# The modulation products of a two-block transformer step: matrix-vector work moved from TensorE to GpSimd between the feed-forward tiles

## The reference, cut to what matters

```
sh_l, sc_l, g_l = split(silu(c)     @ w_mod[l] + b_mod[l], 3)
sh_c, sc_c, g_c = split(silu(c_ctx) @ w_mod[l] + b_mod[l], 3)
hl = xl * (1.0 + sc_l) + sh_l
```

## Time and profile before

| | |
|---|---|
| median of 3 runs (lowest, highest) | 3065.2 us (3062.55, 3065.78) |
| span of the profiled execution; no other time of its own is given | 3064.5 us |
| TensorE busy in the span | 98% |
| VectorE, ScalarE, GpSimd busy in the span | 54%, 44%, 1% |
| mean granted clock of TensorE | 0.993 of full speed |
| the stage with the up tiles, from the span's start | about 791 us to 1306 us |
| instructions in the span | 48560 |

### The profile page before, as it was taken

How to read it: one execution, slowest core, us unless ns; L and a number is a source line. 1 busy time by engine, 2 the same in 40 slices (tenths; PEclk the granted TensorE clock), 3 DMA queues, 4 the chain that set the end, 5 groups by cost and what they waited for, 6 DMA issues and landing times.

```text
span 3064.5 us, 48560 instructions
## 1 busy us (share of the span) xinstructions
PE 2991.3 (98%) x19912; PEld 2540.5 (83%) x19912; DVE 1668.5 (54%) x2561; ACT 1352.7 (44%) x2084; POOL 43.7 (1%) x84
## 2 busy tenths in 40 slices
PE   8999999999899999999999999999999999999997
PEld 7888876898688888788888887788888998889996
DVE  6666666443766666664463325554563564257754
ACT  5333334434455555454453224444442562255543
POOL 1000000000000000000000000000000000000000
PEclk9999999999999999999999999999999999999998
DMA  7666655446766666745552222222233442234442
GB/s 255 231 212 216 220 192 216 139 163 264 272 232 220 220 234 249 279 160 187 180 184 97 94 85 83 83 79 88 88 132 110 165 165 83 97 123 149 152 157 105
DMA packets 73800, 510.18 MB, mean 166 GB/s; under 512 B 8325, under 2 KB 8465, under 8 KB 19601
## 3 DMA queue, kind: packets, MB, share of 16 engines
q1 hardware_dynamic: 63504, 435.74, 41.4%
q0 software_dynamic: 10112, 71.73, 5.8%
HBM read 503.23 MB, written 6.55 MB: 166 GB/s over the span
## 4 chain that ended last, share of the span: by engine, by line
PE 93%; DVE 4%; ACT 1%; DMA 1%; issue 0%; SPq 0%; ACTq 0%; DVEq 0%
PE bank L777 21%; PE bank L721 16%; PE bank L720 8%; PE bank L1500 6%; PE bank L1502 6%; PE bank L1501 6%; PE bank L920 3%; PE bank L921 3%; PE bank L922 3%; PE bank L952 2%; PE bank L1060 2%; PE bank L818 2%; PE bank L819 1%; PE bank L820 1%; PE bank L1127 1%; PE bank L1538 1%
## 5 line engine op out<-in xcount | busy, mean ns | idle before, releaser
L2322 DVE TENSOR_TENSOR ring_f32r<-ring_f,high_f32r 128x1024 fp32r<-128x1024 f32 (+1 forms) x738 | 830.1, 1162 | 751.7 <-ACT high_f32r L1675 728.1
L1675 ACT CAST high_f32r<-ring_f 128x1024 fp32r<-128x1024 f32 (+1 forms) x644 | 609.4, 995 | 836.8 <-PE bank L777 461.4
L721 PE MATMUL bank<-hyz_f32r,high_f32r 128*128 128x512 f32 x2112 | 743.4, 398 | 1.0 <-DVE hyz_f32r L2322 1.0
L720 PE MATMUL bank<-hyz_f32r,ring_f32r 128*128 128x256 f32 x2008 | 562.6, 280 | 3.0 <-DVE hyz_f32r L2322 2.0
L777 PE MATMUL bank<-hyz_f32r,high_f32r 128*128 128x512 f32 (+1 forms) x2016 | 536.7, 343 | 4.3 <-DVE hyz_f32r L2322 2.1
L721 PEld LDWEIGHTS bank<-hyz_f32r,high_f32r 128*128 128x128 f32 x2112 | 391.8, 188 | 101.7 <-issue 15.3
L777 PE MATMUL bank<-hyz_f32r,ring_f32r 128*128 128x512 f32 (+1 forms) x1184 | 411.8, 348 | 0.0
L777 PEld LDWEIGHTS bank<-hyz_f32r,high_f32r 128*128 128x128 f32 x2016 | 349.9, 191 | 48.1 <-issue 2.8
L720 PEld LDWEIGHTS bank<-hyz_f32r,ring_f32r 128*128 128x128 f32 x2008 | 378.9, 189 | 8.5 <-DVE hyz_f32r L2322 2.7
L1500 PE MATMUL bank<-hyz_f32r,high_f32r 128*128 128x512 f32 (+1 forms) x1024 | 359.3, 351 | 3.0 <-DVE ring_f32r L2322 3.0
L1502 PE MATMUL bank<-hyz_f32r,ring_f32r 128*128 128x512 f32 (+1 forms) x1024 | 344.8, 337 | 0.0
(11 more groups left out here) (417 smaller groups left out, 4073.4 us busy)
## 6 DMA issues: line engine op xcount, KB each, us to landing
ring_f<-in_w_in SPq DMA_DIRECT2D x159, 1024.0 KB, 4.9
ring_f<-in_w_up SPq DMA_DIRECT2D x88, 1024.0 KB, 4.9
ring_f<-in_w_out SPq DMA_DIRECT2D x56, 1024.0 KB, 4.9
ring_f<-in_w_mod SPq DMA_DIRECT2D x48, 1024.0 KB, 4.9
ring_f<-in_w_down SPq DMA_DIRECT2D x64, 704.0 KB, 4.1
h_f<-in_w_mod POOLq DMA_DIRECT2D x34, 1024.0 KB, 7.5
ring_f<-in_w_kv SPq DMA_DIRECT2D x8, 1024.0 KB, 5.4
z_f<-in_w_mod POOLq DMA_DIRECT2D x8, 1024.0 KB, 7.7
```

Source lines behind the costliest of these rows:

```text
L720: mm(small, lo, x_hi, start=False, stop=False)
L721: last = mm(bank, hi, pair(x_hi, x_lo), start=start, stop=stop)
L1675: act.copy(w_hi[p % 2][:, half], slot[s % SLOTS][:, half]).then_inc(w_high, 1)
L2322: return v.tensor_tensor(out, in0, in1, op)
```

## The change

GpSimd multiplies the slabs of groups 5 and 4, in that order, by the condition value of their partition and adds them up in SBUF. Group 5 is made for one stream, group 4 for both. For the first slab of a stream GpSimd writes the 128 x 2048 product into the sum. For each of the 15 others it does, for each half of 1024 columns, one multiplication into `mod_part` (`Z[:, 40:44]`) and one addition into the sum, each behind a semaphore wait for the instruction before. That is 61 instructions a stream, 183 in all. It issues the load of slab n+2 when slab n has been used. The sums lie where the context's tokens will be loaded (`X1_AT`), so that load moves from the first turn to behind the last product. TensorE then adds a finished sum over the partitions with four matmuls for each stream (`pool_summed`), behind tile 28 for group 5 and behind tile 82 for group 4. The second stream of group 4 starts once the sum of group 5 has been read. VectorE before its work for tile 80, and ScalarE before it casts the second part of the feed-forward activations, wait for the last product.

```diff
-UP_MODS = [4 + 7 * k for k in range(8)] + [62 + 3 * k for k in range(8)]
+UP_SUMMED = (28, 82)
+POOL_GROUPS = (5, 4)
+POOL_STREAMS = {5: 1, 4: 2}
+POOL_MADE = (1 + 15 * 4, 1 + 15 * 4 + 2 * (1 + 15 * 4))
...
+        mod_acc = {5: [arena[:, X1_AT:X1_AT + SLOT]],
+                   4: [arena[:, X1_AT + SLOT:X1_AT + 2 * SLOT], arena[:, X1_AT:X1_AT + SLOT]]}
+        mod_part = Z[:, 40:44].rearrange("p t n -> p (t n)")
+        sum_sel = arena[:, SIZE - 576:SIZE - 512]
...
-            for n in range(NORM_MODS, 48, 2):
-                pool.wait_ge(S("mod_read"), 48 + n)
-                pool.wait_ge(S("up_mod_loaded"), 16 * (n - 4))
-                for m in range(2):
-                    load(up_mod[m], d["w_mod"][48 + n + m, :, :], "up_mod_loaded")
-                if n == NORM_MODS:
-                    load(x_all[:, KC * T:], d["ctxT"], "rows_loaded")
...
+                for s, acc in enumerate(mod_acc[g]):
+                    if g == 4 and s == 1 and k == 0:
+                        pool.wait_ge(S("mod_read"), 48 + NORM_MODS + 1)
+                    if k == 0:
+                        nc.gpsimd.tensor_scalar(acc, up_mod[n % 2], mod_c[:, k, s:s + 1], None, ALU.mult).then_inc(S("mod_pool"), 1)
+                        made += 1
+                        continue
+                    for half in (slice(0, SLOT // 2), slice(SLOT // 2, SLOT)):
+                        pool.wait_ge(S("mod_pool"), made)
+                        nc.gpsimd.tensor_scalar(mod_part, up_mod[n % 2][:, half], mod_c[:, k, s:s + 1], None, ALU.mult
+                                                ).then_inc(S("mod_pool"), 1)
+                        pool.wait_ge(S("mod_pool"), made + 1)
+                        nc.gpsimd.tensor_tensor(acc[:, half], acc[:, half], mod_part, ALU.add).then_inc(S("mod_pool"), 1)
+                        made += 2
+                pool.wait_ge(S("mod_pool"), made)
+                if n + 2 < len(slabs):
+                    up_slab(n + 2)
+            pool.wait_ge(S("mod_read"), 48 + NORM_MODS + 2)
+            load(x_all[:, KC * T:], d["ctxT"], "rows_loaded")
...
+            def pool_summed(turn):
+
+                g = POOL_GROUPS[turn]
+                pe.wait_ge(S("mod_c"), 4)
+                pe.wait_ge(S("mod_pool"), POOL_MADE[turn])
+                pe.wait_ge(S("mod_row"), 4 + turn)
+                for n, acc in enumerate(mod_acc[g]):
+                    for m in range(4):
+                        last = mm(bk[4][32 * m:32 * m + 32, :], sum_sel[:, 31 - n:63 - n], acc[:, m * 512:(m + 1) * 512],
+                                  start=(n == 0), stop=(n == POOL_STREAMS[g] - 1))
+                last.then_inc(S("mod_read"), 1)
...
-                if j in UP_MODS:
-                    n = NORM_MODS + 2 * UP_MODS.index(j)
-                    pe.wait_ge(S("up_mod_loaded"), 16 * (n - 2))
-                    for m in range(2):
-                        up_mod_matvec(48 + n + m, up_mod[m])
+                if j in UP_SUMMED:
+                    pool_summed(UP_SUMMED.index(j))
...
+            dve.wait_ge(S("mod_pool"), POOL_MADE[1])
+            for j in range(4):
+                up(80 + j, 0)
```

More of the change, by code:

```diff
@@ L621, in _ @@
             pool.wait_ge(S("rows_loaded"), 96)
-            for n in range(NORM_MODS, 48, 2):
-                pool.wait_ge(S("mod_read"), 48 + n)
-                pool.wait_ge(S("up_mod_loaded"), 16 * (n - 4))
-                for m in range(2):
-                    load(up_mod[m], d["w_mod"][48 + n + m, :, :], "up_mod_loaded")
-                if n == NORM_MODS:
-                    load(x_all[:, KC * T:], d["ctxT"], "rows_loaded")
+            pool.wait_ge(S("mod_read"), 48 + NORM_MODS)
+            slabs = [(g, k) for g in POOL_GROUPS for k in range(KC)]
@@ new lines, in up_slab @@
+            def up_slab(n):
+                g, k = slabs[n]
+                pool.dma_start(up_mod[n % 2], d["w_mod"][g * KC + k, :, :]).then_inc(S("rows_loaded" if n % 2 else "up_mod_loaded"), 16)
+            up_slab(0)
+            up_slab(1)
+            nc.gpsimd.memset(sum_sel, 0.0).then_inc(S("mod_c"), 1)
+            pool.wait_ge(S("mod_c"), 3)
+            nc.gpsimd.memset(sum_sel[:, 31:32], 1.0).then_inc(S("mod_c"), 1)
+            made = 0
+            for n, (g, k) in enumerate(slabs):
+                if n % 2:
+                    pool.wait_ge(S("rows_loaded"), 96 + 16 * (n // 2 + 1))
+                else:
+                    pool.wait_ge(S("up_mod_loaded"), 16 * (12 + n // 2 + 1))
+                for s, acc in enumerate(mod_acc[g]):
[15 more added lines that the diff above has]
+                    up_slab(n + 2)
@@ L1413, in up_mod_matvec @@
             def up_mod_matvec(n, slab):
-                if n % KC == 0 and n > 48:
-                    pe.wait_ge(S("mod_row"), n // KC)
                 mod_matvec(n, 4, slab)
+            def pool_summed(turn):
[8 more added lines that the diff above has]
+                last.then_inc(S("mod_read"), 1)
             norms = iter(range(NORM_MODS))
@@ L1848, in mod_row_copied @@
             def mod_row_copied(g, bank, row):
-                act.wait_ge(S("mod_read"), 16 * (g + 1))
+                act.wait_ge(S("mod_read"), 16 * (g + 1) if g < 4 else 48 + NORM_MODS + g - 3)
                 act.copy(row, bk[bank][:, :]).then_inc(S("mod_row"), 1)
@@ L1853, in mod_copied @@
                 act.wait_ge(S("mod_turned"), g + 1)
-                act.copy(MOD6[:, g, :], bk[bank][:, 0:32]).then_inc(S("mod_out"), 1)
+                group = POOL_GROUPS[g - 4] if g >= 4 else g
+                act.copy(MOD6[:, group, :], bk[bank][:, 0:32]).then_inc(S("mod_out"), 1)
             def a_v_copied(i):
@@ L2047, in act_high @@
                 if part == 1:
-                    act.wait_ge(S("mod_read"), 96)
+                    act.wait_ge(S("mod_pool"), POOL_MADE[1])
                 act.copy(act_hi[part][:, m:m + 4], Z[:, 4 * n:4 * n + 4]).then_inc(S("act_high"), 1)
@@ L2757, in _ @@
                         act_low(j)
-            with dve.Fori(0, 5) as i:
+            with dve.Fori(0, 4) as i:
                 for j in range(4):
                     up(64 + j, i)
+            dve.wait_ge(S("mod_pool"), POOL_MADE[1])
+            for j in range(4):
+                up(80 + j, 0)
             for j in range(4):
@@ L2787, in _ @@
                 step(ts(part, part, 1.0, op0=ALU.add))
-            dve.wait_ge(S("rows_loaded"), 112)
+            dve.wait_ge(S("rows_loaded"), 96 + 16 * KC + 16)
             dve.wait_ge(S("down_used"), 3 * 15 + 2)
```

## The result

The changed kernel takes 3235.3 us (median of 4 runs, 3229.7 to 3236.4) against 3063.9 for the kernel before beside it. The ratio is 1.0556, with a 95% interval of 1.0543 to 1.0569: 171 us slower. Forecast were 3245 us and a range of 3060 to 3335.

The account below looks back on a forecast made before the run. TensorE was taken as the bound, busy 98% of 3064.5 us. Taking off 28.4 for its relief and adding 210 for GpSimd holding VectorE gave 3246, stated as 3245 us; range 3060 to 3335.

Parts of the forecast that it names:

- The bound and the relief: TensorE sets the stage's pace; sixteen turns (31.3 us) go, twelve matmuls (2.9) are added: net -28.4 us.
- Interference decides: In the stage, VectorE or GpSimd stands still while the other reads SBUF: +210 us, chance 0.58.
- The product's duration: GpSimd's product of 1024 columns, bounded at 0.95 to 1.8 us from memsets, taken as 1.2.
- The growth of a tile: VectorE's tile grows from 5.15 to 9.1 us while GpSimd works, 63 tiles at 3.45 us over 5.65: +216.
- The prediction's dearer figure, 11.25: Tile time in us if GpSimd also gets between VectorE's subtraction halves: 45 tiles x 5.6 = +252 us.
- GpSimd itself is late: Rival: GpSimd misses tiles 28 and 80 without touching VectorE; at 5.5 us a pair about 3090; chance 0.05.
- the upper bound of a pair: GpSimd's dearest product plus sum with allowances, 1.8 + 2.66 + 0.4 = 4.86 us, just in time.
- my own sign of being wrong: TensorE waiting at `pool_summed` would mean GpSimd was the one held; no size given.
- the prediction's deadlines: GpSimd has 5.0 us a pair until tile 28, then 4.8 us a pair until tile 80.
- My single term for interference: VectorE held by GpSimd's instructions in the stage: +210 us, near the lower of the middle figures +216 and +252.
- The rival of shared reads: GpSimd and VectorE share SBUF reads instead of stopping: +40 to +110, 3076 to 3146, about 3105 us; chance 0.20.
- No interference: Rival: GpSimd and VectorE don't touch each other, so only TensorE's relief counts: 3036 us, faster; chance 0.17.

Follow-up runs that it names:

- no arithmetic: Changed kernel without GpSimd's products and sums but each stream's first product, 45 one-column memsets instead; loads, waits and TensorE's twelve matmuls kept: 3033.3 us, ratio 0.9900.
- the gated one: Kernel before with only group 5 on GpSimd, in 512-column pieces, each sum waiting for VectorE's second subtraction: 3052.3 us, ratio to before 0.9957.
- sums only: Changed kernel without the products behind the first of each stream (one more made to fill the operand), 90 sums kept: 3182.3 us, ratio to before 1.0380.

## Why the prediction was right, and where it was not

**The bound and the relief: right.** A turn at 1.96 us and twelve matmuls kept gave 28.4 us; with no arithmetic it measured 31.

**Interference decides: right.** In the timelines shown a subtraction of VectorE and a sum of GpSimd overlap by 0.13 us at most. The Trainium skill ("SBUF — State Buffer", section "Who interferes with whom") says that the second of the two to start fully blocks, and the traces agree for the sums (a subtraction beginning in a sum ends 1.09 us behind it) but not for the products as the page words it: they cost a pair of subtractions 0.7 to 0.85 us of their 2.84, and the taps at 1113.35 nothing.

**The product's duration: wrong, and outside its bounds.** I put it between 0.95 and 1.8 us from the memset's rate; it is 2.84 undisturbed. The sum, 2.34, is near the 2.2 taken. The Trainium skill ("GPSIMD Engine Reference", section "Elementwise — side-by-side cycle accounting") led to an estimate of 2.25 for the sum, and the trace comes within 4% of it. Pairs therefore take 5.37 us, not 3.8, and need one tile each.

**The growth of a tile: too large.** I had 9.1 us with every instruction of VectorE that has two SBUF inputs held by products and sums alike; it is 7.27. Products hardly hold, so a tile meets one sum, which costs 5.15 + 2.1 = 7.3 us. GpSimd works for some 80 tiles in place of 63, without the stretch at 5.65 between two slow ones that I had expected. (The prediction's dearer figure, 11.25, leaves out the tenth that it takes off the other one; with it the tile would be 10.6 and the price +244 in place of +252. Its upper end of 3335 lies midway between +252 and +347, which it doesn't say.)

**"GpSimd itself is late": underrated.** It had a chance of 0.05, because the upper bound of a pair was 4.86. It happened on top of the interference, which I had treated as exclusive with it. TensorE waits 19.1 us at tile 28 and 51.1 through VectorE at tile 80; the run with the first sum four tiles later showed that these are one debt. TensorE waiting at `pool_summed` was my own sign of being wrong, "which means GpSimd was the one held", and it came. GpSimd was indeed held as well: 0.94 us for each product and 0.45 for each sum, 126 us over the 90 pairs. From its first product at 802.6 to its last sum, which ends at 1452.7, lie 650 us: 90 undisturbed pairs (483), three long products (16), the issues of the loads, which I had put at nothing (some 25), and these 126. Lateness alone would not have done it: by the prediction's deadlines an undisturbed pair with its share of the issues, 5.8 us in group 5 and 5.6 in group 4, is late by 25 + 49 us, an estimate that gives 3110.

**The sum: near by luck.** From 202.5 us: 97 in VectorE's waits in the tiles, 51 at tile 80, 19 at tile 28, and 34.6 because TensorE's own matmuls take longer in the records (lines 757 and 758, which the down projection uses too: 568.8 + 770.2 us against 563.4 + 741.0 with no arithmetic). These make 202. The 34.6 have two parts. The lower clock is one. These two matmuls follow the stand at tile 28, the first at the lower level and the second at the higher:

```profile
1023.50 0.63 PE L758 MATMUL bank<-hyz_f32r,high_f32r 128*128 128x512 f32 x1
1025.32 0.39 PE L758 MATMUL bank<-hyz_f32r,high_f32r 128*128 128x512 f32 x1
```

TensorE was busy for 34 us of this stage in stretches granted about 0.5, of which half, 17 us, are lost. The restarts are the other part. In sixteen tiles at full clock, with 16 waits, TensorE is busy 94.25 us, where sixteen tiles of 5.65 take 90.4, or 0.24 us for each wait, some 16 us for 68:

```profile
1092.79:1209.30 116.51, 94.25 (x514) 78.23 (x513) 95.84 (x89) 47.47 (x77) 112.63 (x37) 1.00 0.49 180
```

My single term for interference was 210. Some 5 us of the clock's share follow the two stands, so interference proper is about 127 and lateness about 75. The first was too large by 83 and the second left out, and only their near equality put the total within 10 us.

**The rival of shared reads** has something for it in the products; the sums exclude it. **No interference** is excluded by every run with sums but the gated one.

## What to carry to other kernels

Before giving GpSimd element-wise work, count VectorE's instructions with two SBUF inputs and its slack in each turn of the loop: a two-input instruction of GpSimd, here a sum of 1024 columns, cost VectorE nearly its whole length wherever they met. A sum shorter than one of VectorE's gaps was nearly free when the semaphore at the gap's beginning started it. And when two unrelated causes could each slow a kernel (held, late), don't treat them as alternatives: price them together.

## What the runs showed of the hardware that was not expected

A GpSimd product by a scalar from SBUF, with one tensor input, is slower than a two-input sum: 2.84 us against 2.34 for 128x1024 float32, and at 512 columns at least 1.55 against 1.28. It holds VectorE only for a part of that. The long product of 2048 columns, 5.45 us undisturbed, holds more. In the run with sums only it stands beside a pair of subtractions (GpSimd first):

```profile
1010.92 6.49 POOL L651 TENSOR_SCALAR x_f<-h_f,rest_f 128x2048 f32<-128x2048 f32 x1 [98.27 <-PE bank L1464]
```

```profile
1010.96 5.80 DVE L2369 TENSOR_TENSOR ring_f32r<-ring_f,high_f32r 128x1024 fp32r<-128x1024 f32 x2
```

The pair takes 5.80 us in place of 2.36, so it lost 3.44, and the product itself takes 6.49 in place of 5.45. With 1024 columns the product started 0.27 us ahead of the pair at 1008.49 and cost it 0.7 (0.28 and 0.85 for the other pair shown). So VectorE goes on 1.0 to 1.1 us behind the start of a product of 1024 columns and 3.5 behind that of 2048: in all three cases 1.7 to 2.0 us of the product's undisturbed length hold nothing; why, these runs don't show.

TensorE's clock fell not only at the two long stands. With sums only TensorE is busy 337 of the 437 us from 803 to 1240, and the granted clock there is 0.86 in the mean, while the changed kernel has 0.96 with 350 busy. The waits differ in length: 23 of up to 7.1 us there (99.8 us in all), against waits of at most 3.0 in the changed kernel's tiles. That the length decides is not shown.
